# Idle products and reordered weight loads around the modulation units, and one activation table with a Newton step in the odd layer

## What is computed

```
for i in range(DEPTH):                               # DEPTH = 2
    mod_l = silu_c  @ w_mod[i] + b_mod[i]            # 1024 -> 6 * 1024
    mod_c = silu_cc @ w_mod[i] + b_mod[i]
    ul = modulate(rms_norm(hl, norm_mix_g[i]), sh1_l, sc1_l)
    uc = modulate(rms_norm(hc, norm_mix_g[i]), sh1_c, sc1_c)
    # i = 0: Fourier groups and a bidirectional state-space scan
    # i = 1: windowed attention and neighbourhood attention;
    #        q and k are normed per head: rms_norm(q, g), rms_norm(k, g)
    hl = hl + g1_l * ol
    hl = hl + g2_l * sq_relu_mlp(modulate(rms_norm(hl, norm_ff_g[i]), sh2_l, sc2_l), w_ff1[i], w_ff2[i])
    # the same for hc in layer 0
```

## Time and profile before

| | |
|---|---|
| three runs | 1275.67 us median (1275.34 to 1278.98) |
| the profiled execution | 1275.35 us, its span 1273.6 us |
| busy: TensorE products / weight loads | 1208.5 us (95%) / 961.8 us (76%) |
| busy: VectorE / ScalarE / GpSimd | 807.6 us (63%) / 600.2 us (47%) / 86.5 us (7%) |
| mean granted clock of TensorE | 0.989 |
| transfers | 166.38 MB, mean 131 GB/s |

### The profile page before, as it was taken

One profiled execution on the slowest core, in us unless ns is written; L12 is line 12 of the kernel. 1 busy time (PEld: TensorE's weight loads), 2 busy tenths in 40 slices (PEclk: granted clock), 3 DMA queues, 4 the chain that ended last, 5 costly groups with the idle time before them and its releaser, 6 DMA issues.

```text
span 1273.6 us, 17426 instructions
## 1 busy us (share of the span) xinstructions
PE 1208.5 (95%) x6554; PEld 961.8 (76%) x6554; DVE 807.6 (63%) x1153; ACT 600.2 (47%) x1009; POOL 86.5 (7%) x73
## 2 busy tenths in 40 slices
PE   5799899999998999999999999999989899999998
PEld 3466678787876787687887887885778559888997
DVE  3554488796977564677576675695542795645555
ACT  4531264655647332732331331423978784845543
POOL 0000101002020005000000000044000003000000
PEclk9799999999999999999999999999999999999999
DMA  9457021211121224253453443541233103355554
GB/s 366 199 227 284 38 67 51 67 50 65 53 67 34 66 93 167 104 187 125 173 198 132 173 173 132 198 148 66 83 133 116 34 1 134 125 190 184 185 192 150
DMA packets 41839, 166.38 MB, mean 131 GB/s; under 512 B 4528, under 2 KB 6704, under 8 KB 38704
## 3 DMA queue, kind: packets, MB, share of 16 engines
q1 hardware_dynamic: 41488, 164.97, 36.8%
q10 hardware_dynamic: 288, 0.56, 0.1%
HBM read 164.46 MB, written 1.05 MB: 130 GB/s over the span
## 4 chain that ended last, share of the span: by engine, by line
PE 71%; DVE 14%; ACT 7%; issue 4%; DMA 3%; DVEq 0%; SPq 0%; ACTq 0%
PE ps L1652 47%; PE ps L1659 8%; PE ps L1917 7%; DMA mring<-in_w_mod 2%; DVE cacc L1365 2%; PE ps L1675 1%; DVE sm L1600 1%; ACT ey L1081 1%; ACT u L977 1%; DVE ey L1439 1%; PE ps L1742 1%; DVE prob L1625 1%; ACT w_hi L927 1%; DVE macc L1524 1%; DVE mixF L1465 1%
## 5 line engine op out<-in xcount | busy, mean ns | idle before, releaser
L1216 DVE TENSOR_TENSOR w_lo<-raw,w_hi 128x1024 fp32r<-128x1024 f32 x206 | 258.1, 1253 | 131.3 <-ACT w_hi L927 130.9
L927 ACT ACTIVATE w_hi<-raw 128x1024 fp32r<-128x1024 f32 x206 | 216.6, 1053 | 236.1 <-DMA raw<-in_w_ff 177.9
L1652 PE MATMUL ps<-a_hi,w_hi 128*128 128x512 f32 (+1 forms) x868 | 319.7, 368 | 0.4 <-DVE w_lo L1216 0.4
L1652 PE MATMUL ps<-a_hi,w_lo 128*128 128x512 f32 (+1 forms) x868 | 308.2, 355 | 0.0
L1652 PE MATMUL ps<-a_lo,w_hi 128*128 128x512 f32 (+1 forms) x868 | 308.2, 355 | 0.0
L1652 PEld LDWEIGHTS ps<-a_hi,w_hi 128*128 128x128 f32 x868 | 164.9, 190 | 28.9 <-issue 4.0
L1652 PEld LDWEIGHTS ps<-a_lo,w_hi 128*128 128x128 f32 x868 | 164.9, 190 | 25.3 <-issue 1.2
L1652 PEld LDWEIGHTS ps<-a_hi,w_lo 128*128 128x128 f32 x868 | 164.7, 190 | 23.3
L1652 PE MATMUL ps<-b_hi,w_hi 128*128 128x512 f32 x304 | 119.5, 393 | 0.0
L1652 PE MATMUL ps<-b_lo,w_hi 128*128 128x512 f32 x304 | 118.6, 390 | 0.0
L1652 PE MATMUL ps<-b_hi,w_lo 128*128 128x512 f32 x304 | 118.3, 389 | 0.0
(11 more groups left out here) (253 smaller groups left out, 1701.6 us busy)
## 6 DMA issues: line engine op xcount, KB each, us to landing
raw<-in_w_ff SPq DMA_DIRECT2D x128, 512.0 KB, 3.5
mring<-in_w_mod SPq DMA_DIRECT2D x24, 1024.0 KB, 7.6
mring<-in_w_mod SPq DMA_DIRECT2D x32, 768.0 KB, 5.0
raw<-in_w_in_even SPq DMA_DIRECT2D x36, 512.0 KB, 3.5
raw<-in_w_in_odd SPq DMA_DIRECT2D x18, 512.0 KB, 3.4
raw<-in_w_out_even SPq DMA_DIRECT2D x16, 512.0 KB, 3.5
raw<-in_w_out_odd SPq DMA_DIRECT2D x8, 512.0 KB, 3.5
bias<-in_rpb_na SPq DMA_DIRECT2D x8, 256.0 KB, 3.8
```

What stands on the lines that cost most here:

```text
L927: nc.scalar.activation(w_hi[:, u % RING, :, :], raw[:, u % RING, :, :], ACT.Copy).then_inc(hi_done, 1)
L1216: v.tensor_tensor(w_lo[:, u % RING, :, :], raw[:, u % RING, :, :], w_hi[:, u % RING, :, :].bitcast(F32), ALU.subtract).then_inc(lo_done, 1)
L1652: ins = mm(out_ap, w_[:, n % RING, k, :], (x_[k][:, 0:ntok] if type(x_) is list else x_[:, k, 0:ntok]), start=(k == 0 and j == 0), stop=(k ...
```

## The change

It moves and adds steps in the script and changes what a few steps do:

- the opening has three idle products behind each of the units 5, 6 and 7 and four behind the column products; the three weight loads stand behind all eight units; "wsplit" 1 is gone, unit 0 is split between the row copy and the first tile (VectorE: ahead of it), and unit 1 behind the second tile of NORM0;
- "prime" fetches the units 8 to 10, and each later "mu" step fetches the unit three further on, behind a wait that this step's own unit is used;
- MOD_AFTER lies up to one or two products earlier;
- the second half of each dftw goes to bank B_Y;
- the warm-up Ln of the norms is a table preload, and the first hstat preloads a table that has both Ln and Exp;
- hnorm takes one Newton step on ScalarE's result (four more VectorE operations and one rearranged, with a scratch tile in u32), and the bank of a statistic is freed by VectorE's reading of it (hv_done).

Two hunks that only add the name hv_done to the list of semaphores are left out.

```diff
--- before.py
+++ after.py
@@ -64,7 +64,7 @@
 MI1 = NMOD // (MG1 * QUADS)
 MR1 = 4
 MOD_WITH = (0, 1, 2, 4, 5, 7, 9, 11, 13, 14)
-MOD_AFTER = (0, 2, 4, 6, 8, 9, 11, 12)
+MOD_AFTER = (0, 2, 4, 5, 7, 8, 10, 11)
 MOD_ROW, MOD_COL, MOD_ADD = 14, 15, 15


@@ -174,10 +174,10 @@
             s += [("xin", f) for f in range(len(X_BANKS), KT)]
         if 1 <= k <= 4:
             s += [("xnt", 2 * k - 2), ("xnt", 2 * k - 1)]
-        if k >= KT - LEAD:
-            s.append(("wload", k - (KT - LEAD)))
-    s += [("wsplit", u) for u in range(AHEAD)]
-    s += [("mrow", 0), ("mcol", 0), ("prime",), NORM0]
+        elif k > 4:
+            s.append(("turn", k, 3))
+    s += [("wload", u) for u in range(LEAD)]
+    s += [("mrow", 0), ("mcol", 0), ("prime",), ("wsplit", 0), ("turn", 3, 4), NORM0]

     def gemm(kind, i):

@@ -421,7 +421,7 @@
         elif st == NORM0:
             pass
         elif k == "turn":
-            b = (B_SEG, B_SEG, B_TR)[st[1]]
+            b = (B_SEG, B_SEG, B_TR, X_BANKS[3])[min(st[1], 3)]
             job(st, b, freed=last[b], filled=last[b])
         elif k == "norm":
             n_sq += 1
@@ -436,7 +436,7 @@
             job(st + ("tot",), B_AUX[0], freed=("dtx_done", 3))
         elif k == "dftw":
             for q in range(2):
-                job(st + (q,), B_AUX[0], freed=("vf_done", 2 * st[1] + q + 1))
+                job(st + (q,), (B_AUX[0], B_Y)[q], freed=("vf_done", 2 * st[1] + q + 1))
         elif k == "dfts":
             n_mix += 1
             job(st, B_TR, freed=("mix_done", n_mix))
@@ -454,8 +454,7 @@
         elif k == "cb":
             job(st, B_AUX[0])
         elif k == "hstat":
-            n_var += 1
-            job(st, B_AUX[n_aux % 2], freed=("var_done", n_var))
+            job(st, B_AUX[n_aux % 2], freed=("hv_done", nk))
             n_aux += 1
         elif k == "seg":
             job(st, B_SEG)
@@ -800,13 +799,20 @@
                     sp.wait_ge(*slot_free(u))
                 sp.dma_start(raw[:, u % RING, :, :], src).then_inc(raw_in[u % RING], 16)

+            def fetch(n):
+                g, kk = n // KT, n % KT
+                if n >= MR0:
+                    sp.wait_ge(mu_used, n - MR0 + 1)
+                sp.dma_start(mring[:, n % MR0, :], mod_rows(0, kk, QUADS * MI0 * P * g, QUADS * MI0 * P)).then_inc(mod_in[n % MR0], 16)
+
             for st in steps:
                 if st[0] == "mu":
                     _, g, kk = st
                     n = KT * g + kk
-                    if n >= MR0:
-                        sp.wait_ge(mu_used, n - MR0 + 1)
-                    sp.dma_start(mring[:, n % MR0, :], mod_rows(0, kk, QUADS * MI0 * P * g, QUADS * MI0 * P)).then_inc(mod_in[n % MR0], 16)
+                    if g == 0:
+                        fetch(n)
+                    elif n + MR0 < MU0:
+                        fetch(n + MR0)
                 elif st == ("xsq",):
                     for t in range(NCH):
                         src = (x, ctx)[t // 2][0, P * (t % 2):P * (t % 2) + P, :]
@@ -814,6 +820,8 @@
                 elif st == ("prime",):
                     sp.dma_start(wdt[:, :, :], w_dt).then_inc(wdt_in, 16)
                     sp.dma_start(c0[:, C0_A:C0_W], consts0[:, C0_A:C0_W]).then_inc(dft_in, 16)
+                    for n in range(KT, KT + MR0):
+                        fetch(n)
                 elif st[0] in ("wload", "gemm"):
                     for g in loads[st]:
                         load(unit[g], source(g[1], g[2]))
@@ -952,13 +960,15 @@
                         for i in range(2):
                             nc.scalar.activation(u32[:, f % 2, SEQ * i:SEQ * i + SEQ], xnT[:, f, SEQ * i:SEQ * i + SEQ], ACT.Identity,
                                                  bias=mod[:, 0, f, i:i + 1], scale=coefA[:, f, i:i + 1]).then_inc(signal(xu_done if i else act_seq), 1)
+                        if f == 1:
+                            high(1)
                 elif k == "norm":
                     ntok = SEQ if st == ("norm", 1, "ff") else T
                     act.wait_ge(h_done, h_before[st])
                     nc.scalar.activation(sq[:, 1, 0:ntok], hT[:, KT - 1, 0:ntok], ACT.Square).then_inc(signal(sq_done), 1)
                     b = jobs[st][0]
                     act.wait_ge(consts_set, 2)
-                    nc.scalar.activation(warm[:, 0:1], eps[:, 0:1], ACT.Ln).then_inc(signal(act_seq), 1)
+                    act.preload_act_table_set("natural_log")
                     act.wait_ge(*filled(st))
                     nc.scalar.activation(sq[:, 1, 0:ntok], ps[:, b, 0:ntok], ACT.Ln, scale=1.0 / D, bias=eps[:, 0:1]).then_inc(signal(var_done), 1)
                     act.wait_ge(*latest())
@@ -1094,13 +1104,15 @@
                     act.wait_ge(*latest())
                     nc.scalar.activation(gate[:, XT - 1, :], gate[:, XT - 1, :], ACT.Exp, scale=-0.5).then_inc(signal(rstd_done), 1)
                 elif k == "hstat":
+                    if qk_n[st[1:]] == 0:
+                        act.preload_act_table_set("natural_log_exp_and_others")
                     if qk_n[st[1:]] >= 2:

                         act.wait_ge(qn_done, qk_n[st[1:]] - 1)
                     b = jobs[st][0]
                     act.wait_ge(*filled(st))
                     nc.scalar.activation(rms_of(st), ps[:, b, 0:odd_tokens[st[1:]]], ACT.Ln, scale=1.0 / HD,
-                                         bias=eps[:, 0:1]).then_inc(signal(var_done), 1)
+                                         bias=eps[:, 0:1]).then_inc(signal(act_seq), 1)
                     act.wait_ge(*latest())
                     nc.scalar.activation(rms_of(st), rms_of(st), ACT.Exp, scale=-0.5).then_inc(signal(hs_done), 1)
                 elif k == "mixsplit":
@@ -1248,8 +1260,6 @@
                     dve.wait_ge(silc_done, 1)
                     dve.wait_ge(consts_set, 3)
                     v.tensor_copy(sil32[:, :, 0:2], silc[:, :, :]).then_inc(signal(sil_done), 1)
-                elif k == "wsplit":
-                    low(st[1])
                 elif k == "mcol":
                     j = st[1]
                     b = jobs[st][0]
@@ -1275,11 +1285,14 @@
                     dve.wait_ge(*latest())
                     v.scalar_tensor_tensor(out=coefA[:, :, :], in0=mod[:, 0, KT:2 * KT, :], scalar=1.0,
                                            in1=gmixT[:, 0, :].unsqueeze(2).broadcast_to([P, KT, 2]), op0=ALU.add, op1=ALU.mult).then_inc(signal(coef_done), 1)
+                    low(0)
                     for f in range(KT):
                         dve.wait_ge(xu_done, f + 1)
                         v.tensor_copy(a_hi[:, f, :], u32[:, f % 2, :]).then_inc(signal(u_done), 1)
                         dve.wait_ge(u_done, f + 1)
                         v.tensor_tensor(a_lo[:, f, :], u32[:, f % 2, :], a_hi[:, f, :].bitcast(F32), ALU.subtract).then_inc(signal(split_done), 1)
+                        if f == 1:
+                            low(1)
                 elif k == "norm":
                     L = st[1]
                     ntok = SEQ if st == ("norm", 1, "ff") else T
@@ -1564,8 +1577,20 @@
                     dve.wait_ge(hs_done, qk_n[st[1:]] + 1)
                     dve.wait_ge(qraw_done, qk_n[st[1:]] + 1)
                     x_ = ktile(*st[1:])
+                    key = ("hstat",) + st[1:]
+                    r_, b = rms_of(key), jobs[key][0]
+                    c_ = u32[:, 0, 0:odd_tokens[st[1:]]]
+                    if qk_n[st[1:]]:
+                        dve.wait_ge(qn_done, qk_n[st[1:]])
+                    v.tensor_tensor(c_, r_, r_, ALU.mult).then_inc(signal(dve_seq), 1)
+                    dve.wait_ge(*latest())
+                    v.scalar_tensor_tensor(out=c_, in0=ps[:, b, 0:odd_tokens[st[1:]]], scalar=HD * EPS, in1=c_, op0=ALU.add, op1=ALU.mult).then_inc(signal(hv_done), 1)
                     v.scalar_tensor_tensor(out=x_, in0=x_, scalar=vt[:, 2, g_q[st[1]]:g_q[st[1]] + 1],
-                                           in1=rms_of(("hstat",) + st[1:]), op0=ALU.mult, op1=ALU.mult).then_inc(signal(qn_done), 1)
+                                           in1=r_, op0=ALU.mult, op1=ALU.mult).then_inc(signal(dve_seq), 1)
+                    dve.wait_ge(hv_done, qk_n[st[1:]] + 1)
+                    v.tensor_scalar(c_, c_, -0.5 / HD, 1.5, ALU.mult, ALU.add).then_inc(signal(dve_seq), 1)
+                    dve.wait_ge(*latest())
+                    v.tensor_tensor(x_, x_, c_, ALU.mult).then_inc(signal(qn_done), 1)
                 elif k == "rot":
                     x_ = ktile(*st[1:])[:, 0:SEQ]
                     b = jobs[st][0]
```

(4 more changed lines are left out.)

## The result

The changed kernel takes 1255.95 us (median of 6 runs, 1254.95 to 1256.65), the kernel before 1275.51 us in the 6 runs beside it (1273.94 to 1278.98). The ratio is 0.9844, 95% interval 0.9831 to 0.9857: 19.9 us faster, with 18.2 to 21.6 us inside the interval. The forecast of 1253.0 asked for 22.6 us. The direction and most of the sizes came out; one term, the opening, did not.

A forecast was written before the change was run, and what follows sets the result against it. It took a string of TensorE products (71% of the chain) as the bound, with gaps and half clock to win. Terms 4.9 + 5.5 + 0.7 + 4.2 + 3.5 + 3.5 + 0.3 = 22.6 us gave 1253.0 us, range 1249 to 1258.

The forecast's parts named there:

- The opening: Start to unit 8: weights behind modulation and idle products holding the clock end the pair at 51.3, gain 4.9 us.
- Rival (c): Opening gains nothing because weight 0 arrives after the row copy, or unit 9 is late; 2.5 to 4 us, chance 0.10.
- The unit behind the pair: Modulation units behind the pair: fetching ahead removes a 3.8 us wait and half clock, gain 5.5 us.
- Fourier products: A second bank removes four waits for VectorE's copy of the first half, gain 4.2 us, other end 3.
- The last pass: Fourth pass of MLP 0: earlier multiply-adds remove the row product's 2.1 us wait and slow clock, gain 3.5 us.
- rival (b): Last pass of MLP 0: multiply-add wait stays as VectorE steps beside GpSimd's squares take longer; 3.5 us, chance 0.07.
- The odd layer: Without ScalarE's table loads the duplication's wait for the v copy and slow clock shrink, gain 3.5 us.
- (d): Odd layer: table loads stay because each function asks for its own table; 1257.5 us, chance 0.05.
- (e): Odd projections: VectorE becomes the bound, its added 27 us lie open; 1283.5 us, chance 0.02.
- Norms: Three norms: a table preload replaces a 0.2 us dummy activation on the chain, gain 0.3 us.
- Rival (a): Opening: idle products don't hold the clock, or it falls again in the pair's start; 2 to 4.5 us, chance 0.13.

The follow-up runs named there:

- a2: The kernel after with one idle product instead of three behind units 5 to 7, two instead of four behind the column products: 1252.14 us.
- b3: The kernel before with only the modulation units fetched ahead (8 to 10 at "prime", each later one three ahead): 1270.23 us.
- c1: a2 with the dt weights split at the end of NORM0's step instead of behind the fifth unit's copy: 1252.14 us.
- b2: The kernel before with only the second half of each dftw put in another bank: 1268.55 us.
- b4: The kernel before with only the odd layer's part (common table, Newton step, hv_done), norms keeping their warm-up: 1269.78 us.
- b1: The kernel before with only the new MOD_AFTER: 1274.24 us, ratio 0.9992.
- a6: The kernel after without the Newton step, common table kept, statistic's bank freed by ScalarE's Ln again: 1256.29 us.
- a1: The kernel after without any idle product in the opening, weights still behind the modulation: 1257.44 us.
- a3: The kernel after without the three idle products between unit 7 and the column products: 1254.64 us.
- a5: The kernel after without the preload of the common table, Newton step kept: 1263.16 us.

## Why the prediction came out as it did

**The opening: the step that failed.** "Three idle products of 0.43 us each (24 took 10.30 us)" is wrong by a factor of two. The 24 in the chain are entries, and a float32 product is two of them: the 12 products of that step in the script took 10.30 us, 0.86 us each. By the Trainium skill (TensorE: Matmul & The Clock Gate, "What happens when you issue a matmul") one column enters the array per clock, an estimate of 0.21 us for 512 columns at 2.4 GHz; the rows show twice that for an entry and four times for such a product. So the three fill 2.84 us and not 1.3 us of a gap that the transfers open only for 1.5 us, each unit is late by 1.3 us, and the columns by 1.9 us. The rest of that paragraph stood: the clock was held, 1 MB arrives in 2.5 us (a2), column and unit products halved, and with a filling that fits the gap unit 8 starts at 51.53, forecast 51.3. Of the transfers' 2.5 us a2 shows 1.7 (unit 7 at 33.44 for 35.15), or 2.6 counted from unit 5. The term was 4.9 us and the kernel after got 0.4 (1.3 counted from unit 5). I gave "0 to 1 us" as the other end, with the wrong reason for it (a clock not held). Rival (c) named this result too, likewise for a reason that isn't there: ScalarE had split weight 0 (37.66 to 38.71) before the columns began at 39.71, and unit 9 was not late.

**The unit behind the pair.** 5.5 us came as worked out. The sentence "it is needed two products (11 us) later, so I cost it at nothing" failed by 0.9 us: I counted only the copy of that unit itself, and not the small split of the dt weights that stands behind it on ScalarE and is needed at once. It is 3.0 us in b3 and 2.7 us in a2. The earlier the pair ends, the more of it is open, so a part of any gain in the opening is given back here. c1 shows the cure in the trace.

**Fourier products.** 4.2 and 0.7 us were forecast and 6.0 came: the waits of 4.2 and 0.7, and 1.0 us because products behind a wait are slower. The next wait, for vf, stays (0.8 us before, 0.9 after).

**The last pass.** The mechanism is right, and rival (b) falls. Three of the eight steps of that pass lie beside GpSimd's squares and take 4.3 to 4.4 us instead of 3.54; with the old schedule (b2) it is four steps. VectorE's last one in the kernel after:

```profile
845.78 4.31 DVE L1537 SCALAR_TENSOR_TENSOR macc<-mring,silc,macc 128x1536 f32<-128x1536 f32 x2
```

It ends at 850.1, 3.7 us ahead of the row product's 853.8. VectorE is slower beside GpSimd, as the rule cited in the prediction has it, and here TensorE doesn't wait for it. The size is 2.1 us and a remnant of 1.6 us that was in the one profile and not in b2, b3 and b4; the median saving of b1 (1.0 us, at most 2.2) is nearer to the wait alone.

**The odd layer.** 4.1 us for 3.5. The wait for the v copy went from 2.7 to 0.9 us, near the 0.7 us worked out, the slow stretch went in this execution, and rivals (d) and (e) fall with a6 and the one table load that is left. The 1.7 us that the prediction took for the slow stretch are again a remnant that not every execution has. b3 waits 2.7 and 0.8 us like the kernel before, and its stretch is 103.59 us, not 105.21. From 950 to 975 us, before and in b3 (in b3 the first wait ends at 947.77, and from 925 to 950 its clock reads 1.00 too):

```profile
950.00:975.00 25.00, 23.62 (x102) 18.47 (x103) 6.82 (x9) 16.97 (x23) 0.00 (x0) 0.93 0.33 108
```

```profile
950.00:975.00 25.00, 25.00 (x117) 20.13 (x116) 6.96 (x8) 19.59 (x26) 0.00 (x0) 1.00 0.36 121
```

So 2.5 us of the 4.1 are what the change gives where neither execution has a slow stretch. **Norms**: 0.3 us were forecast. The second norm shows 0.1 us (its stretch is 101.23 us in b4, without the preload, and 101.12 to 101.16 in a1, a3, a6, c1 and the kernel after); at the other two no gain is shown. The -0.6 us of the last row are no gain of the change: b1 to b4, with the old code there, read 278.6 to 278.9 us.

**In all**, errors of +4.5 (opening) and +0.9 (dt weights) stand against -1.1, -0.2, -0.6, -0.3 and -0.1 of the other terms, 3.1 us short up to the last product. Behind it the kernel after is 0.4 us shorter, which makes the 19.9 us of the spans. That the total came within 3 us of the forecast is partly luck: some of the terms that came out larger (the pass, the odd layer, the last row) owe it to slow stretches of the one profile of before. Rival (a) fell too: the clock read 1.00.

## What to carry to other kernels

Count a filler by the products of the script and the time of its whole group, never by the entries of the profile, and size it below the gap that the slowest supplier leaves: here one product kept the clock and three made the opening 4 us longer. When a load moves back in a queue, follow every consumer behind the waiting copy on its engine, not only the consumer of that load. An operation that is free beside the products may be free only thanks to the other half of the change, so run the halves apart.

## What the runs showed of the hardware that was not expected

**The same wait does not always cost clock.** The duplication waits 0.9 and 0.8 us in both the kernel after and a2, as it waited 2.7 and 0.8 us in both the kernel before and b3. TensorE's stretch from the first of the two waits on, in the kernel after and in a2:

```profile
933.00:938.50 5.50, 4.41 (x24) 3.13 (x25) 3.24 (x6) 1.10 (x2) 0.00 (x0) 1.00 0.39 140
```

```profile
930.90:936.40 5.50, 4.71 (x14) 2.95 (x15) 2.92 (x5) 0.80 (x1) 0.00 (x0) 0.70 0.36 131
```

One reads 1.00 and the other 0.70 after gaps of the same length, and the stretch to the first scores is 37.5 or 39.1 us by it. With the row product above this is the second place where one profile alone would misprice a wait by 1.6 us. A third lies behind the Fourier products: from the first product with xbc to the idle products, b3, b4 and a5 read 364.6 to 364.7 us and all other kernels 363.0 to 363.1 us. Such stretches are a likely cause for medians of four runs that wander by 1 to 2 us; whether they are the whole cause is open. The idle products of the opening do not steady the time: a1, without them, ranges over 4.5 us in four runs, a2, with one, over 5.6 us.
